# Moving the SBUF start addresses of the buffers that the fp32r products read

## The reference

```python
x = x + 0.5 * swiglu(rmsnorm(x, ffn1_norm), w_gate, w_up, w_down)      # width 2816
x = x + hybrid_mixer(...)          # NSA and forgetting attention, gates, w_up_nsa, w_up_fox, w_out
x = x + memory_cross_attention(...)                                    # w_q, w_kv, w_o: 1024 x 1024 each
x = rmsnorm(x + 0.5 * swiglu(...), final_norm)                         # second ffn, width 2816
# second block
x = x + rwkv7_time_mix(rms_norm(x, ln_mix[0]))                         # r, k, v, output, low-rank parts
x = x + square(relu(rms_norm(x, ln_mlp[0]) @ w1)) @ w2                 # width 4096
x = x + swa_layer(rms_norm(x, ln_mix[1]), k_sh, v_sh)                  # q, output; window attention
x = x + square(relu(rms_norm(x, ln_mlp[1]) @ w1)) @ w2                 # width 4096
```

## The kernel before

| activations | form | matmuls | remainder of activations | of the split weights |
|---|---|---|---|---|
| hidden (4 stages) | row | 2592 | 160 | 224 |
| hT | col, row | 4992 | 128 | 224 |
| o_parts | col | 192 | 32 | 224 |
| y_turned (on gates_ab, and on a second buffer in the memory stage) | row | 384 | 32 | 224 |
| memT | col | 192 | 32 | 224 |
| mixed_keys (on AR) | col | 192 | 32 | 224 |
| mixed_hi / mixed_lo | col | 192 | 192 / 32 | 224 |
| o_swa | row | 192 | 224 | 224 |
| hT / memT / mixed, stationary, tile moving | natural | 144 / 192 / 192 | 128 / 32 / 192 and 32 | 224 |

## Time and profile before

### The profile page before, as it was taken

The page is one execution under the profiler, slowest core; times in us unless marked ns, Lnnn a source line. Parts: engine busy times, 40 slices in busy tenths (PEclk is TensorE's granted clock), DMA queues, the critical chain, the costliest instruction groups (busy, mean ns, idle before and its releaser), DMA issues. The chain is left out here.

```text
span 1482.1 us, 28884 instructions
## 1 busy us (share of the span) xinstructions
PE 1408.5 (95%) x12748; PEld 1351.0 (91%) x12748; DVE 951.4 (64%) x1303; ACT 714.4 (48%) x1100; POOL 7.1 (0%) x12
## 2 busy tenths in 40 slices
PE   7999999998999899999889978998999997989999
PEld 7999999887899899999889977888999985889999
DVE  4655666479674456566678864666666679566565
ACT  5444455356464445444538423444444565454443
POOL 0000000000000000000000010000000000000000
PEclk9999999999999999999989986999999997999999
DMA  6555545640445335555424300024455441235542
GB/s 261 204 200 194 180 164 200 232 167 30 168 148 197 115 128 179 207 174 196 171 71 162 142 3 31 30 84 145 171 196 203 171 143 57 86 143 186 209 174 86
DMA packets 33109, 222.48 MB, mean 150 GB/s; under 512 B 3879, under 2 KB 5295, under 8 KB 6616
## 3 DMA queue, kind: packets, MB, share of 16 engines
q1 hardware_dynamic: 31928, 219.57, 41.2%
q10 hardware_dynamic: 1056, 1.07, 0.2%
HBM read 219.54 MB, written 1.07 MB: 149 GB/s over the span
## 5 line engine op out<-in xcount | busy, mean ns | idle before, releaser
L304 DVE TENSOR_TENSOR tile_lo<-ring,tile_hi 128x1024 fp32r<-128x1024 f32 x396 | 476.3, 1223 | 290.9 <-ACT tile_hi L294 289.8
L294 ACT ACTIVATE tile_hi<-ring 128x1024 fp32r<-128x1024 f32 x396 | 408.7, 1054 | 281.0 <-PE ps L346 276.9
L344 PE MATMUL ps<-hT_hi,tile_hi 128*128 128x256 f32 x1664 | 473.3, 284 | 11.3 <-DVE hidden_lo L761 7.6
L346 PE MATMUL ps<-hT_hi,tile_lo 128*128 128x256 f32 x1664 | 469.0, 282 | 0.0
L345 PE MATMUL ps<-hT_lo,tile_hi 128*128 128x256 f32 x1664 | 468.9, 282 | 0.0
L344 PEld LDWEIGHTS ps<-hT_hi,tile_hi 128*128 128x128 f32 x1664 | 316.5, 190 | 18.5 <-DVE hidden_lo L761 8.0
L345 PEld LDWEIGHTS ps<-hT_lo,tile_hi 128*128 128x128 f32 x1664 | 316.6, 190 | 0.0
L346 PEld LDWEIGHTS ps<-hT_hi,tile_lo 128*128 128x128 f32 x1664 | 316.2, 190 | 0.0
L344 PE MATMUL ps<-hidden_hi,tile_hi 128*128 128x256 f32 x864 | 238.7, 276 | 0.0
L345 PE MATMUL ps<-hidden_lo,tile_hi 128*128 128x256 f32 x864 | 238.7, 276 | 0.0
L346 PE MATMUL ps<-hidden_hi,tile_lo 128*128 128x256 f32 x864 | 238.5, 276 | 0.0
(11 more groups left out here) (459 smaller groups left out, 2120.7 us busy)
## 6 DMA issues: line engine op xcount, KB each, us to landing
ring<-stream SPq DMA_DIRECT2D x204, 1024.0 KB, 4.8
x_sb<-x SPq DMA_DIRECT2D x4, 256.0 KB, 4.0
bias<-f_dram ACTq DMA_DIRECT2D x1, 1024.0 KB, 8.1
fox_bias<-forget_dram SPq DMA_DIRECT2D x1, 1024.0 KB, 6.3
squares<-mem SPq DMA_DIRECT2D x1, 1024.0 KB, 4.8
out<-x_sb SPq DMA_DIRECT2D x4, 256.0 KB, 2.4
const_sb<-const SPq DMA_DIRECT2D x1, 577.0 KB, 9.5
small_sb<-small SPq DMA_DIRECT2D x1, 493.5 KB, 9.7
```

The lines of the kernel that those rows point to most:

```text
L294: act.activation(e.w_hi[:, n % SPLIT, :], e.ring[:, tile % RING, span(n % 2, HALF)], ACT.Copy).then_inc(e.tile_hi.handle, 1)
L304: dve.tensor_tensor(e.w_lo[:, n % SPLIT, :], e.ring[:, CUT[n // 2] % RING, span(n % 2, HALF)], e.w_hi[:, n % SPLIT, :].bitcast(F32), ALU.s ...
L344: pe.matmul(out, left[0], right[0], start=start, stop=False)
L346: return pe.matmul(out, left[1], right[0], start=False, stop=stop)
```

## The change

A constant `LINE = 256` and three places modulo it are added: 224 for the split weights, 160 for the moving activations, 160 for `hT`. `sb` gets an argument `place`; where it is given, a pad tensor is allocated first, so that the tensor begins at that remainder. `pair` passes 160 by default, so that `hidden`, `memT`, `kvT`, `o_swa` and the others made by it are placed. `o_parts`, `gates_ab` (and with it `y_turned`), the rwkv buffers made by `big`, `AR` (and `mixed_keys`) and `mixed_hi` are given 160 as well. `hidden` and the split weights had these remainders before. Nothing that is issued, no wait and no order changes; all addresses behind a pad move up, by 32 to some hundred bytes.

```diff
+LINE = 256
+AT_WEIGHTS, AT_MOVING, AT_INPUT = 224, 160, 160
...
-        def sb(stack, name, shape, dtype=F32):
+        def sb(stack, name, shape, dtype=F32, place=None):
             start = -(-(SBUF_END - nc.sbuf_bytes_remaining) // 32) * 32
+            if place is not None and (place - start) % LINE:
+                pad = (place - start) % LINE
+                stack.enter_context(nc.sbuf_tensor(f"{name}_pad{nc.next_id()}", [P, pad // 4], F32))
+                start += pad
             tensor = stack.enter_context(nc.sbuf_tensor(name, shape, dtype))
...
-        def pair(stack, name, shape):
-            return tuple(sb(stack, f"{name}_{part}{nc.next_id()}", shape, F32R) for part in ("hi", "lo"))
+        def pair(stack, name, shape, place=AT_MOVING):
+            return tuple(sb(stack, f"{name}_{part}{nc.next_id()}", shape, F32R, place) for part in ("hi", "lo"))
...
-        e.hT = pair(ctx, "hT", [P, KC, SEQ])
+        e.hT = pair(ctx, "hT", [P, KC, SEQ], AT_INPUT)
...
-        e.w_hi, e.w_lo = pair(ctx, "tile", [P, SPLIT, HALF])
+        e.w_hi, e.w_lo = pair(ctx, "tile", [P, SPLIT, HALF], AT_WEIGHTS)
...
-        outs = e.sb(stack, "o_parts", [P, 16, SEQ], F32R)
+        outs = e.sb(stack, "o_parts", [P, 16, SEQ], F32R, AT_MOVING)
...
-        m.ab = e.sb(stack, "gates_ab", [P, 2 * KC, SEQ])
+        m.ab = e.sb(stack, "gates_ab", [P, 2 * KC, SEQ], F32, AT_MOVING)
...
-        big = lambda where, *names: (e.sb(where, name, [P, KC, SEQ]) for name in names)
+        big = lambda where, *names: (e.sb(where, name, [P, KC, SEQ], F32, AT_MOVING) for name in names)
...
-            w.AR = e.sb(inner, "AR", [P, PAIRS, TT, 2, P])
+            w.AR = e.sb(inner, "AR", [P, PAIRS, TT, 2, P], F32, AT_MOVING)
...
-                w.mixed = (e.sb(first, "mixed_hi", [P, KC, SEQ], F32R), e.over("mixed_lo", w.before, [P, KC, SEQ], F32R))
+                w.mixed = (e.sb(first, "mixed_hi", [P, KC, SEQ], F32R, AT_MOVING), e.over("mixed_lo", w.before, [P, KC, SEQ], F32R))
```

## The result

The changed kernel takes 1466.81 us, the median of ten runs from 1457.58 to 1478.72; the kernel before, beside it, 1484.14 us (ten runs, 1480.16 to 1489.74). The ratio is 0.9887, with a 95% interval from 0.9857 to 0.9917: faster by 17.3 us. The forecast was 1459 us. Two things are to be explained: the 8 us that are missing in the median, and the spread, 21 us against 10 us before. Nothing in the change looks as if it could make a kernel less steady.

A forecast was written before the change was run, and what follows sets the result against it. TensorE's pace from matmul to matmul was taken as the bound, set by operand addresses modulo 256. Terms 1 to 3 gave 27.0 us, deductions left 24: span 1458, median 1459 us; range 1452 to 1465, extended to 1470 for 8 of 10.

The forecast's parts named there:

- Nothing changes: Rival for the whole kernel: the address remainder only stands in for something else `hidden` has; 1483 us, chance 0.06.
- Term 1: 4992 matmuls on `hT`, moved from 128 to 160, gain 4.2 ns each: 21.0 us.
- Terms 2 and 3: `o_parts`, `y_turned`, `memT`, `mixed_keys` gain 4.0 us, `mixed` 0.8 us; `o_swa`, from 224 to 160, gains 1.2 us.
- Term 4: 528 natural-form matmuls (activations stationary), taken at 117.8 ns: sum 0, bounds -2.5 and +0.8 us.
- Term 5: Other engines: ScalarE and VectorE unchanged; small fp32 recurrence matmuls taken as 0, 1 us allowed either way.
- the cover: Where TensorE never idles, what is late next has room: VectorE's 60% becomes 62%, the weight queue is held by buffers.
- The other two deductions: Taken off the gain: 1.0 us for time at halved clock, 0.9 us for attention-stage `hT` bursts ending in waits.
- the settling: Deduction: after each of some sixty breaks the pace needs a few matmuls to settle; 1 us.
- the third rival: Feed-forward stages starting slow at 160 draw `hidden` in, costing 10.9 us with no gains: 1494 us, chance 0.08.
- Only part of it: After waits some stretches settle in the slow pace, half the gain lost: about 1470 us (1465 to 1478), chance 0.12.
- Slower: With `hT` and `hidden` at one remainder, a stage starting slow keeps `hidden` slow: 1494 us, chance 0.08.

The follow-up runs named there:

- The control: Changed kernel with the lo weights at 96 and `hT` back at 128: 1477.95 us, ratio 0.9950 to the kernel before.
- the streams alone: Separate kernel without the reference's work: column, natural and burst matmul streams beside traffic, lo weights at 96, some natural ones at 224; 401.19 us.
- the second profile of after: The changed kernel, unaltered, run and profiled again in a later comparison: median 1467.96 us, ratio 0.9875 to the kernel before.
- the second kernel of streams: Separate kernel of matmul streams at 224/160, started after waits, quiet then with traffic, then hi and lo at different places; 910.05 us.
- the first kernel of streams: Separate kernel of matmul streams with nothing beside them, weights at 224, 0 or 128 against activations at eight places; 856.65 us.

## Why the prediction was right or wrong

**The sign and the mechanism hold.** The kernel is faster, the time lies in the range, and the pace goes with the two addresses modulo 256; with no other work present the paces of the earlier trace rows come back at the same places. "Nothing changes" is refuted. The rule that stood against the sum, in the Trainium skill, "TensorE: Matmul & The Clock Gate" (Step-by-step), that a weight load takes nothing from the running matmul because the ports are independent, does not cover this: in a kernel with nothing else running, the same instructions take 113.3 to 120.0 ns by the place of the operands alone. All streams here load weights for each matmul, so no run shows that it is the loads that take the time.

**The terms of the sum were sized right.** Term 1, `hT`, said 21.0 us. The control comes near, with hardly a draw in it: lo weights at 96 with `hT` at 160 and at 128, 0 and 22.6 us above the line. Its `hT` runs at 118.0 ns, not the 117.8 of before, and 0.8 us of it is `hidden`, 2592 x 0.3 ns. Terms 2 and 3 said 6.0 us: with the lo weights at 96 the buffers that they name gain 0.8 (`o_parts`), 1.6 (`y_turned`), 0.7 (`memT`), 1.5 (`mixed`, `mixed_keys`) and 1.1 (`o_swa`), 5.7 us in all, by their mean steps before (117.8, `o_swa` 119.9) and there (113.6). Term 4 took 117.8 ns for the natural form by the mirror of `o_parts`; the streams alone give 117.8 (22 of 24; in the first profile of after `memT` natural has a mean step of 117.2 ns, before 115.7, and `hT` natural 116.3, before 119.9). Where all starts are fast, the step is what was said: in the second profile of after 96 matmuls on `hT` from 55.76 to 66.64, 10.88 us, and a gated step 16.32 us (forecast: 10.9 and 16.4). Term 5 and the cover hold too: VectorE's and ScalarE's busy times are unchanged, and the weight queue still waits for VectorE, 1169.5 us (1182.7). In sum: the profiled execution of before lies 24.6 us above the line (its span and 1.3 us, at clock 0.961), that of 96 lies 0.5 below; 25.1 us between them, which is 27.0 less the 1.9 of the other two deductions, an estimate good to a microsecond or two. But that execution was a good one: the medians of before lie 29.7 to 31.3 us above the line. A gain counted from its rows was some 5 us short of what a kernel with one pace gains in the median, and this hid part of the next error.

**The step that failed** is the settling. The prediction took 1 us for it: "after each break (some sixty) the pace needs a few matmuls to settle". It does need a few; but what it settles to is one of two paces 4.5 ns apart, and it keeps it. In the median run of after that costs 12.7 us above the line (the middle of 9.1 and 16.2) where 1 was allowed. The other two deductions were not tested apart. The argument for the small number stands under the third rival: `hidden` was entered at different phases and always came out fast, so "a place that catches every such entry should catch a start after a wait as well". Those entries were no starts. Each came out of a running stream on `hT` at 128, without a gap, and in before no stream with difference 64 in this form began at a break. The rows could not show what a start does. The one form in which they could, `memT` natural, had two paces, and the text said so, and gave it 0.12.

**The rivals were the mechanism.** "Only part of it" said that after a wait some stretches settle in the slow pace, 1465 to 1478 us: the median 1466.8 lies there, just above the forecast's own 1452 to 1465. "Slower" said that a stage once slow stays slow and takes `hidden` along: that is the first feed-forward stage of the first profile, 152.5 us against 150.0. It needed all of `hidden` to be so, and none of the gains, to end at 1494; the slowest of the ten runs took 1478.7. The two should not have been told apart by a place that catches or doesn't, but by how many draws come out slow. With the 23 of 47 slow starts of the second kernel of streams, and a stage at 6.5 us, the expected loss of four stages is 4 x 6.5 x 0.49 = 13 us, which would have given 1482.8 - 27 + 13 = 1469 us. That this estimate, made afterwards, is near the medians of 1467 and 1468 us is in part luck: in the kernel itself the profiles show one slow stage in twelve, the two squared stages begin at half the granted clock (0.50, steps of 213 ns) and were fast six times of six, and streams outside the stages draw too. The odds of a stage are not known.

## What to carry to other kernels

Where a matmul of 256 columns has its own weight load and TensorE never idles, look at the difference of the two operands' addresses modulo 256: here it moved the pace by up to 6%, and all it took was a pad. If operands come as hi and lo, try different places for the two: a pattern with one stable pace is worth more than one that is fast only if it starts well. And before a pace is taken from a trace for new places, ask whether its rows hold a *start* at these places, or only streams that came from somewhere else; a wide spread of single runs about a line against the clock is the sign of such a choice; the raw spread is not.

## What the runs showed of the hardware

That one pair of addresses has two stable paces, 113.3 ns (steps of 113, 113, 114) and 117.8 ns (117 and 118, now and then 119), was seen in one place of before; that it is settled anew at each start, in a kernel with nothing beside it, was not expected. In many cases the outcome can be read in the first step of the stream. Of the 47 streams at 224/160 that begin at a break in the kernel of starts, all 15 with a first step of 225 to 227 ns went slow, all 13 with 223 or 224 went fast, and of 19 with 220 to 222 eleven went fast. The two profiles of after agree, over the column and row streams of 24 and more that begin at full clock after a break: 226 ns slow three times of three, 223 and 224 fast 13 of 13, 220 to 222 fast 14 of 18, and one with 229 fast. It is no law: ten more streams there begin at a break with first steps of 192 to 195 ns, five fast and five slow, and in the first kernel of streams all nine with 221 or 222 went fast. The break at 36.68 us had 222 ns and went slow; the same break in the second profile had 224 and went fast. So two nanoseconds between the first two matmuls go with 6 us of a stage. What sets these few nanoseconds, no run here tells. Nor is it known why a lo part at the difference 192 takes the choice away; that it does stands on 30 of 30 column streams alone and on two profiles of the whole kernel.
